# Returning the inverted blocks from two queues, and moving one weight load behind them

## The reference

```python
u = rms_norm(h, norm1_g[i])
p_rwkv, p_nsa = jnp.split(u @ w_in[i], [N_RWKV_COLS], axis=-1)
y_rwkv = rwkv7_time_mix(p_rwkv, ...)
y_nsa = nsa_attention(p_nsa, ...)
h = h + jnp.concatenate([y_rwkv, y_nsa], axis=-1) @ w_out[i]
h = h + swiglu(rms_norm(h, norm2_g[i]), ...)

def step(S, inp):                                   # the recurrence, once per token and head
    r_t, w_t, k_t, v_t, a_t, b_t = inp
    sa = jnp.einsum('bhvk,bhk->bhv', S, a_t)
    S = S * w_t[:, :, None, :] + sa[..., None] * b_t[:, :, None, :] + v_t[..., None] * k_t[:, :, None, :]
    return S, jnp.einsum('bhvk,bhk->bhv', S, r_t)
```

## Time and profile before

| | us |
|---|---|
| median of 3 runs | 1437.77 |
| lowest and highest | 1434.64, 1437.98 |
| the profiled execution's own time | 1434.01 |
| its span (first to last instruction) | 1432.2 |
| PE busy in the span | 1400.7 (98%) |
| ACT busy | 690.4 |
| DVE busy | 943.0 |

### The profile page before, as it was taken

How to read it: one execution, slowest core, us unless ns; L and a number is a source line. 1 busy time by engine, 2 the same in 40 slices (tenths; PEclk the granted TensorE clock), 3 DMA queues, 4 the chain that set the end, 5 groups by cost and what they waited for, 6 DMA issues and landing times. The chain is left out here.

```text
span 1432.2 us, 25460 instructions
## 1 busy us (share of the span) xinstructions
PE 1400.7 (98%) x10038; PEld 1289.2 (90%) x10038; DVE 943.0 (66%) x1533; ACT 690.4 (48%) x1106; POOL 82.8 (6%) x136
## 2 busy tenths in 40 slices
PE   8998999999999999999999999999999999999997
PEld 8887888999998999989989999999999988899997
DVE  5765657766667666667467666676666676676665
ACT  6763536433454433376654344443343756643342
POOL 1040010000020000010000000000000113000000
PEclk9999999999999999999999999999999999999999
DMA  9344005655535545524346555364555423464540
GB/s 357 137 168 158 16 1 207 221 179 192 200 133 182 215 176 193 202 77 145 133 177 221 181 198 192 133 221 176 193 199 180 148 89 134 176 221 176 190 161 30
DMA packets 33069, 239.47 MB, mean 167 GB/s; under 512 B 6864, under 2 KB 13280, under 8 KB 14304
## 3 DMA queue, kind: packets, MB, share of 16 engines
q1 hardware_dynamic: 30320, 234.84, 45.3%
q10 hardware_dynamic: 2672, 3.58, 0.7%
HBM read 236.15 MB, written 2.25 MB: 166 GB/s over the span
## 5 line engine op out<-in xcount | busy, mean ns | idle before, releaser
L493 PE MATMUL ps<-uT_h,w_gu 128*128 128x256 f32 x3520 | 614.0, 280 | 0.3 <-DVE w_gu L2007 0.2
L493 PEld LDWEIGHTS ps<-uT_h,w_gu 128*128 128x128 f32 x3520 | 537.8, 188 | 10.9 <-issue 1.4
L493 PE MATMUL ps<-uT_l,w_gu 128*128 128x256 f32 x1760 | 478.8, 279 | 0.0
L493 PE MATMUL ps<-w_dn,h_r 128*128 128x512 f32 x1320 | 326.2, 396 | 0.2 <-DVE h_r L2049 0.2
L493 PEld LDWEIGHTS ps<-uT_l,w_gu 128*128 128x128 f32 x1760 | 325.5, 188 | 0.0
L493 PEld LDWEIGHTS ps<-w_dn,h_r 128*128 128x128 f32 x1320 | 239.3, 188 | 51.3 <-issue 1.7
L1350 ACT CAST w_gu<-ring 128x2048 fp32r<-128x2048 f32 x110 | 210.0, 1909 | 156.3 <-PE ps L493 155.2
L2007 DVE TENSOR_TENSOR w_gu<-ring,w_gu 128x2048 fp32r<-128x2048 f32 x110 | 252.1, 2292 | 35.1 <-ACT w_gu L1350 34.6
L2040 DVE TENSOR_TENSOR us<-ps,bc 128x256 f32<-128x256 f32 x110 | 46.4, 422 | 202.8 <-PE ps L493 202.8
L1363 ACT ACTIVATE wk<-wk 128x256 f32<-128x256 f32 x110 | 46.1, 419 | 261.0 <-DVE wk L2038 261.0
L1356 ACT CAST w_dn<-ring 128x1024 fp32r<-128x1024 f32 x110 | 115.7, 1052 | 82.7 <-PE ps L493 82.6
(11 more groups left out here) (392 smaller groups left out, 1711.1 us busy)
## 6 DMA issues: line engine op xcount, KB each, us to landing
ring<-wstream SPq DMA_DIRECT2D x144, 1536.0 KB, 6.6
cst<-consts_in SPq DMA_DIRECT2D x1, 2185.0 KB, 13.8
wk<-t_row ACTq DMA_DIRECT2D x1, 2048.0 KB, 8.3
wk<-masks_in SPq DMA_DIRECT2D x1, 1216.0 KB, 23.8
x<-x_in SPq DMA_DIRECT2D x2, 512.0 KB, 4.6
ring<-wstream SPq DMA_DIRECT2D x1, 1024.0 KB, 8.9
inh<-gains ACTq DMA_DIRECT2D x2, 512.0 KB, 9.6
out_dram<-x SPq DMA_DIRECT2D x3, 256.0 KB, 2.1
```

Of the source, the lines that this page charges most:

```text
L493: return pe.matmul(o, l, r, start=start, stop=stop, skip_group_check=True)
```

## The change

It issues the returns for the diagonal positions 0, 2, 4, 6 from SP, and those for 1, 3, 5, 7 from ACT, after ACT's `nsa(3)`; ACT waits for `inv_blocks` to be written and for `Mm` to be prepared, as SP does. And it moves the load of slot 11 (the first slot of `w_out`) on SP from before `small_blocks` to behind it.

```diff
                 sp.wait_ge(s["blocks_moved"], MOVED["inverse out"])
                 sp.wait_ge(s["eye_ready"], QUADS)
-                for b in range(8):
+                for b in range(0, 8, 2):
                     d = slice(SMALL * b, SMALL * (b + 1))
                     sp.dma_start(Mm[d, :, d], inv[:, b].rearrange("u r c -> r u c")).then_inc(s["blocks_back"], 16)
 
-            for i in range(RING, 3 * RING):
+            def load(i):
                 sp.wait_ge(s[f"free{i % RING}"], i // RING)
                 sp.dma_start(ring[:, i % RING, :], wstream[i]).then_inc(s[f"land{i % RING}"], 16)
+
+            for i in range(RING, BASE["w_out"]):
+                load(i)
             small_blocks()
+            load(BASE["w_out"])
             with sp.Fori(2, rounds) as r:
...
                 for i in range(1, NSA_FIRST):
                     nsa(i)
+                act.wait_ge(s["blocks_moved"], MOVED["inverse out"])
+                act.wait_ge(s["eye_ready"], QUADS)
+                for b in range(1, 8, 2):
+                    d = slice(SMALL * b, SMALL * (b + 1))
+                    act.dma_start(Mm[d, :, d], inv[:, b].rearrange("u r c -> r u c")).then_inc(s["blocks_back"], 16)
                 i = NSA_FIRST
                 for q in range(len(STEPS)):
                     act.wait_ge(s["P_ps"], q + 1)
```

## The result

The changed kernel takes 1460.24 us (median of 4 runs, 1458.96 to 1463.58), the kernel before 1436.2 (median of 4, 1434.18 to 1437.98). The ratio is 1.0178, 95% interval 1.0163 to 1.0194 (the two medians alone give 1.0167, which lies within it): slower by 24 us, where the sum had said 14.9 and the range of the forecast of 1451 ended at 1456. The profiled execution has a span of 1458.6 us against 1432.2, 26.4 us more.

The account below looks back on a forecast made before the run. PE was taken to bound the kernel, its fillers covering the returns; 0 + 13.4 (wait) + 1.5 (clock) = 14.9 us gave 1448.9 from the profiled execution or 1452.7 from the median; 1451 was taken, range 1440 to 1456.

Parts of the forecast that it names:

- the sum: Whole kernel: 0 for SP's returns, 13.4 for PE's wait and 1.5 for the clock make 14.9 us slower.
- What bounds the kernel now: At PE's wait for the returns: PE bounds, fillers cover the returns by 1.5 us, so earlier landing gains nothing.
- ACT's four returns: After ACT's copy in nsa(3): issued from 131.8 on, last at 133.15, landing at 135.35 in a free system.
- The free system: ACT's returns without loads beside them: last lands 2.2 us after issue, 0.7 us after PE is ready.
- The load of slot 11: On SP behind small_blocks: moving it gains 0; four loads, 6.3 MB, then stand beside ACT's returns.
- How two queues share: DMA engines beside the loads: queues alternate packet by packet whatever the size; returns complete at 148.0, PE loses 13.4 us.
- The rival by which a return's share passes at one turn: ACT's returns beside the loads: last lands at 137.6, PE loses 2.9 us, no clock loss, 1440.7; chance 0.20.
- The wait: PE before its first step: starts at 148.1 instead of 134.65, 13.4 us lost.
- The clock: PE behind its wait: one half-speed stretch of 3.37 us, costing 1.5 us, bounds 0 and 3.4.
- the one example in the earlier trace: Kernel before: after PE was busy 0.62 of 3.0 us, its granted clock was 0.50 for 3.37 us.

Follow-up runs that it names:

- experiment 8: Kernel before the change with 3 instead of 9 fillers in front of PE's wait for the returns: 1433.08 against 1434.07 us, ratio 0.999.
- experiment 3: Changed kernel, but SP waits for all eight returns before loading slot 11 and later ones: 1435.07 against 1434.74 us, ratio 1.0.
- experiment 2: Kernel before with only the load of slot 11 moved, all eight returns on SP: 1434.45 against 1434.74 us, ratio 0.9997.
- experiment 1: Changed kernel with the load of slot 11 back in its old place, so only the returns split: 1455.99 against 1434.74 us, ratio 1.0136.
- experiment 9: Changed kernel with six returns from SP, two from ScalarE inside nsa(3), loads held until all returns land, no stay_busy(9): 1431.88 against 1434.07 us, ratio 0.9983.
- experiment 5: Changed kernel with 16 fillers of 128 columns between PE's wait and the first step: 1454.6 against 1433.82 us, ratio 1.015.
- experiment 10: Changed kernel with 16 fillers of 64 columns between PE's wait and the first step: 1466.36 against 1434.21 us, ratio 1.0223.
- experiment 7: Changed kernel, but SP waits for all returns after issuing the load of slot 11, before later loads: 1447.3 against 1433.82 us, ratio 1.0091.
- experiment 6: Changed kernel with 59 instead of 9 fillers before PE's wait, leaving a short idle time: 1459.45 against 1433.82 us, ratio 1.0189.

## Why the prediction was wrong

Direction, place and the mechanism of the wait were right. The size was not, mainly by the term for the clock: 1451 was forecast, 1460.2 measured. Point by point:

- **What bounds the kernel now** held. PE's fillers covered the returns (experiment 8), so an earlier return could give nothing, and each microsecond beyond the cover was PE's.
- **ACT's four returns** held: issued from 131.61 on, forecast 131.8. The free system was forecast with a loss of 0.7 us and measured with 0.56 (experiment 3).
- **The load of slot 11** held: nothing alone (experiment 2), 4 us through the longer queue (experiment 1, forecast 3.7).
- **How two queues share** held down to the packet: 351 against 352, and a first return that needed until 144.2. The rival by which a return's share passes at one turn is refuted, for pieces of 64 bytes too. The Trainium skill (page "DMA: Bandwidth & Descriptors", section "Queues, rings and completion order") has the engines take turns by whole packets, typically of 9 to 17 descriptors; the turns agree with this case, the size does not, for these transfers: a turn was a single piece. The same page's section "Issuing engines are not separate DMA queues" says that a second issuing engine saves only the sequencer's time; experiments 3 and 9 agree, with a landing of 2.2 us on either queue and a gain of 0.95 us for two issues spared.
- **The wait** was forecast with 13.4 us (PE's start at 148.1) and measured with 15.95 (150.59). Of the difference, 1.45 us is the later start of SP's part in this execution, which made SP's loads that much later while PE was not. The other 1.04 lies in the drain, the time until the loads and the rest of the returns are through: I had worked out 148.2 for the end of the loads and then taken 147.5, plus 0.5 for the rest; nearly all packets had gone by 149.4, and PE followed at 150.6. In experiment 5, where SP's part began 0.06 us from its place in the kernel before, the wait was 14.68, still 1.3 more than forecast.
- **The clock** is the step that failed. "I expect one more such stretch" of 3.37 us, "and I take 1.5", with 3.4 as the upper bound. It was 37.5 us, of which 25 lay under PE's work, and it cost 10.0 us. I had taken the length of the low stretch from the one example in the earlier trace rows, as though it belonged to the clock. It depended on the work: in that example, 16 of the 18 matmuls that PE ran had 128 columns (12 of them filler records), and the clock rose behind them. Behind the new wait stand the steps, mostly with 64 columns. In experiment 5 the clock rose within 16 fillers of 128 columns, in experiment 10 it did not within 16 of 64. With 10 for the clock the sum would have been 23.4, against 24.0 measured by the medians, so this term alone put the measured time above the range. The wait left its own bounds too (149 for the end of the loads), but with 15.9 for it and the 3.4 allowed for the clock the sum would have been 19.3, at most 1 us above the range.

## What to carry to other kernels

A small transfer that somebody waits for should not share the DMA engines with bulk loads from another queue. Here the engines took packets by turns, 64 bytes against 12 KB, and each small piece waited for a large one. Ahead of the loads in the same queue, or issued 1.5 us before the first of them, the returns landed in 2.2 us. Before a wait of PE is priced, look at what PE runs behind it. Here, where these were mostly matmuls of 64 columns, waits of 3 to 16 us each cost about 10 us more in clock, and fillers of 128 columns, in the wait or even behind it, were cheaper. And when a wait is covered by filler work, making it shorter gains nothing until the filler is cut as well.

## What the runs showed of the hardware

- Behind an idle time of 2.9 us PE worked for 34 us at the low clock without a break, and behind one of 3.5 us for 26 us (experiments 7 and 6), while a wait of 0.56 us had no such effect (experiment 3). The low clock ended at last in the midst of the steps. In the changed kernel it rose at 175.5, 1 us behind the only two matmuls of 512 columns in the stretch, here from its timeline:

```profile
172.84 1.91 PE L497 MATMUL ps<-inh,wk 128*128 128x512 f32 x2
```

In experiments 1, 6 and 10 it also rose within 2.5 us of the end of this pair. In experiment 7 it did not: the pair ran at 159.59, and the clock rose at 174.2. What tips it was not tried.
- Behind the long wait, 16 fillers of 128 columns took 5.3 us and the clock rose on the way; 16 of 64 columns took 7.1 and it didn't. The narrow ones took 7.09 / 32 = 0.22 us a record at the low clock; PE's 128-column fillers in the stretch 149.5 to 152.6 of experiment 5 took 3.05 / 14, the same.
- ScalarE's returns were not only taken by turns, they also started late. In the changed kernel, three of the four were issued in the stretch 132 to 135.4, and not one packet of their queue, q10, was moved in it. The view of this stretch has a row for q1 (packets, MB, share) and none for q10, and then the issues (KB each, us to landing):

```profile
q1 hardware_dynamic: 166, 1.10, 96.8%
...
ring<-wstream SPq DMA_DIRECT2D x3, 1536.0 KB, 13.5
wk<-inv_blocks ACTq DMA_DIRECT2D x3, 16.0 KB, 17.4
```

The first packets of ScalarE's queue stand behind 135, and they do so in experiments 1, 5 and 7 too, whether three, four or one load was issued. With the loads held, the whole return took 2.2 us. Why the first packet has to wait so long beside a loaded queue was not tried.
